# The delta rule's inverse: its transposed form made by TensorE transposes that ScalarE drains, the last level over 64 rows, and the steps of the whole kernel in another order

## The chip, the cores and the metric

One program on one core of a Trainium2 chip. The metric is the device time of one execution in microseconds; a time is the median of several executions. The engines are named TensorE (PE in the profile; its weight loads PEld), VectorE (DVE), ScalarE (ACT), GpSimd (POOL) and SyncE (SP, which issues the DMAs).

## The reference

Two blocks of two layers each, on a sequence of 256 rows of 1024 numbers, float32. A layer of block one has one wide projection, an attention branch with a choice of 64 keys, a gated delta rule branch, a gated sum of both and an output projection. Block two has four small attention branches and a layer norm. The change is in the delta rule. Its core, for each head and each chunk:

```python
kb = k * beta[..., None]
lower = jnp.where(strict, jnp.einsum('bhnid,bhnjd->bhnij', kb, k) * decay, 0.0)
tmat = jnp.eye(CHUNK, dtype=jnp.float32) + lower
u = lax.linalg.triangular_solve(tmat, v * beta[..., None], left_side=True,
                                lower=True, unit_diagonal=True)
w = lax.linalg.triangular_solve(tmat, kb * jnp.exp(gc)[..., None], left_side=True,
                                lower=True, unit_diagonal=True)
...
def step(state, xc):
    qk_c, qd_c, kd_c, u_c, w_c, gt_c = xc
    v_new = u_c - jnp.einsum('bhcd,bhde->bhce', w_c, state)
    o_c = (jnp.einsum('bhcd,bhde->bhce', qd_c, state)
           + jnp.einsum('bhij,bhje->bhie', qk_c, v_new))
    state = state * gt_c[..., None, None] + jnp.einsum('bhcd,bhce->bhde', kd_c, v_new)
    return state, o_c
```

There are 8 heads with keys and values of 128. The kernel takes chunks of 128 rows, so it needs the inverse of a unit lower triangular 128x128 matrix for each head, row block and layer: 8 x 2 x 2 = 32 of them.

## The kernel before, in words

Every engine runs one long list of steps. `lanes` writes a list of steps for each lane: "s" loads and splits weights, "m" is the weight matmuls, "a" the delta rule of block one with its norms (the first lane of attentions in block two), "b" the other attention lane, "c" the convolution, "d" and "v" drains of weight tiles, and so on. `ORDER` is a string with one letter for each step, and says from which lane the next step of `PLAN` comes. Each engine walks through the same `PLAN` and does its part of each step, so `ORDER` sets the order on every engine's queue. Waits are on semaphores that count the steps of one kind on one engine.

**Weights.** The weight matmuls are fp32 values split in two: ScalarE rounds a unit of 128x1024 to fp32r (`w_hi`, the helper `A`, line 1278), GpSimd takes the rest (`w_lo`, line 837), and TensorE adds three fp32r products (lines 888, 893 and 900). Their results go to two tiles `bulk` in PSUM, and ScalarE or VectorE drains them. The splits are queued on ScalarE between its other work.

**The chain.** All other work of TensorE writes to two PSUM tiles `chain0` and `chain1`, in turn in the order of the plan (`two_before`). `take(step)` on TensorE waits until the step two before in this order has been drained by the engine that `DRAINER` names. Products of four heads go through `four` (line 977), transposes through `transposes` (line 921, with the identity as the other operand).

**The inverse.** A group g has 4 heads, r is a block of 128 rows. `lt` holds the lower triangular matrices (transposed), `xt` the inverse so far in transposed form and `xx` in plain form. `sub` inverts the blocks of 8 on VectorE, and step x1 (TensorE's transposes, ScalarE's drain) makes `xx` from `xt`. Then four levels n, which join blocks of 8, 16, 32 and 64 (`LEVELS`). In each level invY makes lt*xx on TensorE, and VectorE masks it into `yy` (line 1920). invZ makes two products for each head: the correction of `xx` in columns 0 to 511 of the PSUM tile, and that of `xt` in columns 512 to 1023; VectorE subtracts the one (line 1927) and then the other (line 1929). In the last level only `xt` is needed. The order within a level is Y of both r, then Z of both r. After the last level u, st, ks and o use `xt`: u is the new values, st the state, ks the state's part for the second chunk, o the output. u, st and x1 are drained by ScalarE.

**Around it.** stat and rn norm the rows of q and k, dec makes the decays, kk the products of keys, rep and sub the small inverses. baT, ba_a to ba_c and gc make beta and the summed decays at a layer's start. onorm, mix_b and mix on VectorE and ScalarE follow the last o and give the mixed rows, mT turns them, and the units "o0" and "o1" are the output projection. memT turns the memory input of block two; its DMA is issued by SyncE after o(1,1) of layer 0 was drained (`load_memory`, line 802). In block two, layer 1, the units of the tile h1 run for each half of the rows in an order of their own (`by_half`, `in_turn`).

Of the kernel before, what the change touches and what calls it, by code (L numbers as in the profile page):

```python
# [24 lines left out]
ALU = mybir.AluOpType  # L25
# [3 lines left out]
P = 128  # L29
S = 256  # L30
R = S // P
# [197 lines left out]
def gdn_chain(g):  # L229
# [3 lines left out]
    for n in range(len(LEVELS)):  # L233
        for r in range(R):
            out.append(("invY", g, r, n))
        if n == len(LEVELS) - 1:
            out.append(("kT", g))
        for r in range(R):
            out.append(("invZ", g, r, n))
        if n == 0:  # L240
            out.append(("vT", g))
# [51 lines left out]
def lanes():  # L293
# [20 lines left out]
    "aaaaasamsvamsaasmmsassaaaaacssaccssmmcammcmmcsmasscmscmacamsmcasmssmaadcaasmaassvmamsssbmmacammsmbas"  # L314
    "madsaadsbaamaasmasaaasmaaaasbmamambabsmbsamadsaacsbcbmmsamsscaabmacacscmmascscmsmascammbscamabamcsac"
    "sasamasmdbbammsbmmaxssbmasmmdsbsamssaxsbaaaasdbbmsbbbswmmmaambaaaadwmsbabassmxaamasbbasmsadssabmmbma"
    "madamsawwamwamxsdsabssxsmadmxwxbxaxsbsmmsxxmxmassmvsssvmmmammassaasamasmsdmmssvasaasaccssmmcssmmcamm"
    "mcsamscmcaamcasacsssmmacasasamcmadaamsmavsmmcsasammbbmaaaabsassaasdmaasbdammsaamaasmbsmbsaamsadbmbma"
    "sssaaammsabsmabaacmasacccsmascccbmbsmsmmbbsmbacbsbmamcsaccssmamadaasmasbbamsasssbdmsammmsmsaammmxsaa"
    "dcsbmasassamaxbmwbmamaasbmaadmabsbwsabsasamadasbsdmbmmaaxaasmsaawmbaswmmswaadmsmadsmxxbassxxwxxsxmbb"  # L320
    "ssmmxxssssmmvmvssmaammammdmaasaaammsssssmasdsssmmmsmmmdamasmmamssassaadsdabmsmmasmbbammbbsabmaassdaa"
    "bssmbbmdbsdbsbmamsbvbmambsbsabbsdmmasmdbmsbdsmsbyamsbmmbsymdbbssdydsaymvbsmyysdmymsvydmssdvvsvssvmmm"
    "dmssyssvsssmmmsmmvmymvmvesmsmeesmmmvmmvssmmaaemmmeeaammmmssmssmmassmdmdmssasmsadammsssabmaaammmssbsm"
    "bsddammsbbmabbsmmbsbbsabdsmdbambmsaabmssabbvsambdmabsmbbsmdsbbmsaambmysdmsbdyysmbamysasyvdbdsyydvmmy"
    "ssmvdssmmdvsvmmsmsmvdvsmysmmsvssssmmysvmmsvmeemmevmvmemememm"
# [3 lines left out]
def plan():  # L329
# [17 lines left out]
    "kk": "vector", "rep": "vector", "x1": "scalar", "kT": "vector", "invY": "vector", "invZ": "vector", "vT": "vector",  # L347
# [105 lines left out]
def build(nc, t, out):  # L453
    ctx = ExitStack()
    with ctx:
# [389 lines left out]
        def _(pe):  # L845
            def handlers(p):
# [160 lines left out]
                def invY(g, r, n):  # L1007
# [5 lines left out]
                    four(c, [(lt[:, r, j, :], xx[:, r, j, :]) for j in range(4)]).then_inc(p.done("invY"), 1)  # L1013

                def invZ(g, r, n):
                    c = take("invZ", g, r, n)
                    pe.wait_ge(*p.after("vector", "invY", g, r, n))
                    if n < len(LEVELS) - 1:
                        four(c[:, 0:512], [(xt[:, r, j, :], yy[:, r, j, :]) for j in range(4)])
                    four(c[:, 512:1024], [(yy[:, r, j, :], xt[:, r, j, :]) for j in range(4)]).then_inc(p.done("invZ"), 1)  # L1020
# [228 lines left out]
                def gT(h):  # L1249
# [7 lines left out]
                            invY=invY, invZ=invZ, kq=kq, u=u_, st=st_, ks=ks, o=o_, iT=iT, raw=raw_, qT=qT, kaT=kaT_,  # L1257
# [6 lines left out]
        def _(act):  # L1264
# [15 lines left out]
            def handlers(p):  # L1280
# [14 lines left out]
                def tile_in(name):  # L1295

                    last = max(u for u, x in enumerate(UNITS[p.sec]) if x[0] == name)
# [152 lines left out]

                def u_(g, r):
# [116 lines left out]
                def ln_s(r):  # L1568
                    if r == 0:
# [6 lines left out]
                            stat=stat, rn=rn, dec_b=dec_b, x1=x1, u=u_, st=st_, onorm_a=onorm_a, onorm=onorm, kinorm=kinorm, iT=iT,  # L1576
# [6 lines left out]
        def _(v):  # L1583
            TT, TS, STT = v.tensor_tensor, v.tensor_scalar, v.scalar_tensor_tensor

            def handlers(p):
# [329 lines left out]
                def invY(g, r, n):  # L1916

                    v.wait_ge(*p.after("tensor", "invY", g, r, n))
                    m = cst[:, K_LEVEL + n * P:K_LEVEL + (n + 1) * P]
                    TT(yy[:, r, :, :], heads(half("invY", g, r, n)[:, 0:512]), over(m, 4), ALU.mult).then_inc(p.done("invY"), 1)  # L1920
# [443 lines left out]
```

## Time and profile before

| | |
|---|---|
| median of 3 runs | 1161.22 us (1160.76 to 1161.28) |
| profiled execution | 1163.95 us, span from first to last instruction 1162.1 us |
| granted TensorE clock, mean over the span | 0.979 |
| TensorE busy | 94%, 6482 passes |
| VectorE / ScalarE / GpSimd busy | 59% / 50% / 58% |
| weight matmuls, lines 888 and 900, share of the chain that ended last | 11% and 43% |
| line 977 (`four`), line 921 (`transposes`), share of that chain | 10% and 4% |

How to read it: busy time is a sum of durations with overlaps counted once. TensorE's passes overlap, so the distance between starts, not the duration of one, tells what a pass costs the queue. What stands behind "idle before" is the time that the engine had nothing to run, and what ended it.

### The profile page before, as it was taken

Reading aid. Unit: us, or ns where it says so; the run is one execution under the profiler, and the core shown is the slowest. Engines: PE = TensorE matmul, PEld = TensorE weight load, DVE = VectorE, ACT = ScalarE, POOL = GpSimd, SP = SyncE. Lnnn points to the kernel's source line nnn. Section 1 sums busy time; section 2 is a strip of 40 time slices with the busy share of each in tenths; the row PEclk is TensorE's granted clock in tenths of the full one; section 3 lists DMA queues with packets and bytes.
Section 4 is the critical chain, followed back from the end, with each engine's and each line's share of the span. In section 5 each row is a group of like instructions: output and inputs, shape, how many; then the busy total and the mean of one; then the engine's idle time right before and its main releaser. Section 6 shows DMA issues by size and latency. Waiting matters only on the chain.

```text
span 1162.1 us, 17023 instructions
## 1 busy us (share of the span) xinstructions
PE 1086.8 (94%) x6482; PEld 948.4 (82%) x6482; DVE 684.2 (59%) x1213; ACT 585.9 (50%) x861; POOL 668.7 (58%) x288
## 2 busy tenths in 40 slices
PE   5989999999989999999999998899999879999986
PEld 4978999888868898889988887787887667897865
DVE  3666655787495547546676477506646652665554
ACT  4535145745553465333656275345566433457651
POOL 3746445564466766444765364687445874744584
PEclk9999999999998999999999999999999988999999
DMA  8634334452415554333454332474433554543351
GB/s 277 180 110 141 94 108 118 118 148 78 120 51 196 163 158 143 111 108 110 131 160 127 82 117 93 145 215 121 125 91 109 181 163 145 139 123 107 93 181 55
DMA packets 84447, 152.07 MB, mean 131 GB/s; under 512 B 10576, under 2 KB 16528, under 8 KB 84368
## 3 DMA queue, kind: packets, MB, share of 16 engines
q1 hardware_dynamic: 84368, 151.00, 43.6%
q8 instruction: 52, 0.85, 0.3%
q14 instruction: 27, 0.22, 0.1%
HBM read 149.93 MB, written 1.05 MB: 130 GB/s over the span
## 4 chain that ended last, share of the span: by engine, by line
PE 79%; DVE 10%; ACT 5%; issue 2%; POOL 2%; DMA 1%; POOLq 0%; DVEq 0%; SPq 0%; ACTq 0%
PE bulk L900 43%; PE bulk L888 11%; PE chain L977 10%; PE chain L921 4%; ACT arena L1278 2%; PE bulk L893 2%; POOL w_lo L837 2%; PE chain L1238 1%; PE chain L959 1%; PE chain L1102 1%; ACT w_hi L1278 1%; ACT L1273 1%; PE chain L1219 1%; DVE arena L1758 1%; DVE arena L1671 1%
## 5 line engine op out<-in xcount | busy, mean ns | idle before, releaser
L837 POOL TENSOR_TENSOR w_lo<-raw,w_hi 128x1024 fp32r<-128x1024 f32 (+4 forms) x279 | 654.4, 2361 | 471.5 <-ACT w_hi L1278 471.0
L1278 ACT ACTIVATE w_hi<-raw 128x1024 fp32r<-128x1024 f32 (+4 forms) x279 | 280.1, 1016 | 250.2 <-PE bulk L900 207.8
L900 PE MATMUL bulk<-w_hi,hT_hi 128*128 128x512 f32 (+1 forms) x756 | 308.9, 409 | 13.2 <-DVE arena L1758 7.9
L900 PE MATMUL bulk<-w_hi,hT_lo 128*128 128x512 f32 (+1 forms) x756 | 296.1, 392 | 0.0
L900 PE MATMUL bulk<-w_lo,hT_hi 128*128 128x512 f32 (+1 forms) x756 | 295.6, 391 | 0.0
L900 PEld LDWEIGHTS bulk<-w_hi,hT_hi 128*128 128x128 f32 x756 | 143.6, 190 | 47.8 <-DVE arena L1758 10.7
L900 PEld LDWEIGHTS bulk<-w_hi,hT_lo 128*128 128x128 f32 x756 | 143.0, 189 | 30.4
L900 PEld LDWEIGHTS bulk<-w_lo,hT_hi 128*128 128x128 f32 x756 | 143.8, 190 | 26.7 <-issue 1.2
L977 PE MATMUL chain<-arena 128*128 128x128 f32 x1056 | 131.3, 277 | 5.6 <-ACT arena L1278 3.6
L977 PEld LDWEIGHTS chain<-arena 128*128 128x128 f32 x1056 | 126.2, 192 | 11.3 <-issue 3.9
L888 PE MATMUL bulk<-hT_hi,w_hi 128*128 128x256 f32 x384 | 112.0, 292 | 0.0
L888 PE MATMUL bulk<-hT_hi,w_lo 128*128 128x256 f32 x384 | 110.0, 287 | 0.0
L888 PE MATMUL bulk<-hT_lo,w_hi 128*128 128x256 f32 x384 | 109.8, 286 | 0.0
L1278 ACT ACTIVATE arena<-chain 128x512 f32<-128x512 f32 (+3 forms) x64 | 46.8, 748 | 100.4 <-PE chain L921 72.7
L1273 ACT ACT_TABLE_LOAD x54 | 69.3, 1283 | 45.6 <-DVE tiny L2099 13.5
L921 PE MATMUL chain<-cst,arena 128*128 128x128 f32 (+2 forms) x512 | 72.7, 282 | 20.3 <-DVE arena L1685 11.5
L921 PEld LDWEIGHTS chain<-cst,arena 128*128 128x128 f32 (+2 forms) x512 | 61.4, 146 | 30.6 <-issue 15.1
L888 PEld LDWEIGHTS bulk<-hT_hi,w_hi 128*128 128x128 f32 x384 | 74.9, 195 | 1.1 <-issue 1.0
L888 PEld LDWEIGHTS bulk<-hT_lo,w_hi 128*128 128x128 f32 x384 | 74.9, 195 | 0.0
L888 PEld LDWEIGHTS bulk<-hT_hi,w_lo 128*128 128x128 f32 x384 | 74.8, 195 | 0.0
L1278 ACT ACTIVATE arena<-bulk 128x1024 f32<-128x1024 f32 (+2 forms) x50 | 50.4, 1007 | 47.3 <-PE bulk L900 47.1
L1776 DVE SCALAR_TENSOR_TENSOR arena<-bulk,par,arena 128x253 f32<-128x253 f32 (+2 forms) x144 | 59.4, 475 | 22.5 <-ACT arena L1278 19.4
(244 smaller groups left out, 1378.4 us busy)
## 6 DMA issues: line engine op xcount, KB each, us to landing
raw<-in_w_in_dram SPq DMA_DIRECT2D x194, 512.0 KB, 3.6
raw<-in_w_out_dram SPq DMA_DIRECT2D x32, 512.0 KB, 4.4
raw<-in_w_branch_dram SPq DMA_DIRECT2D x16, 512.0 KB, 3.8
raw<-in_w_mem_kv_dram SPq DMA_DIRECT2D x8, 512.0 KB, 3.8
raw<-in_w_merge_up_dram SPq DMA_DIRECT2D x16, 256.0 KB, 2.7
raw<-in_w_in_dram SPq DMA_DIRECT2D x8, 420.0 KB, 3.3
gain<-in_ln_rows_dram SPq DMA_DIRECT2D x4, 512.0 KB, 5.2
gain<-in_gains_dram SPq DMA_DIRECT2D x3, 512.0 KB, 6.5
```

The lines of the kernel that those rows point to most:

```text
L837: pool.tensor_tensor(lo_of(p, u)[:, 0:n], raw_of(p, u)[:, 0:n], hi_of(p, u)[:, 0:n].bitcast(F32), ALU.subtract).then_inc(p.done("split"), 1)
L888: m = pe.matmul(dst, a, b[:, kk, :], start=(kk == 0 and i == 0 and j % 2 == 0), stop=(kk == tot - 1 and i == 2 and j % 2 == 1), skip_group ...
L893: m = pe.matmul(pair[0:n, 0:S], a[:, k, :], b[:, kk, :], start=(kk == 0 and i == 0), stop=(kk == tot - 1 and i == 2))
L900: m = pe.matmul(dst, a, b[:, k, :], start=(first and k == 0 and i == 0), stop=(last and k == nk - 1 and i == 2))
L921: m = pe.transpose(c[0:n, i * P:i * P + v.shape[0]], v, ident[0:v.shape[0], 0:v.shape[0]])
L959: m = pe.matmul(c[:, r * 4 + j:r * 4 + j + 1], sq[:, j, r * P:(r + 1) * P], ones[:, 0:1], start=(r == 0 and j == 0), stop=(r == 1 and j == ...
L977: m = pe.matmul(c[:, j * P:(j + 1) * P], a, b, start=(j == 0), stop=(j == 3), skip_group_check=True)
L1102: m = pe.matmul(c[:, j * P:(j + 1) * P], pt[qb][:, i * P:(i + 1) * P], pq[:, k, 1280 + kv * P:1280 + (kv + 1) * P], start=(j == 0 and k == ...
L1219: m = pe.matmul(c[:, q * S:q * S + nk], head_T(n, h, 0, slice(qb * P, (qb + 1) * P)), head_T(n, h, 1, slice(0, nk)), start=(q % 2 == 0), s ...
L1273: act.preload_act_table_set(sets[func])
L1278: return act.activation(dst, src, func, **more)
L1776: ins = STT(cv[:, j, back:S], b[:, j * S:(j + 1) * S - back], par1[:, p.l, c:c + 1], cv[:, j, back:S], ALU.mult, ALU.add)
```

## The change

- invZ makes one product for each head instead of two: only `xx` is corrected (levels 0 to 2), and its PSUM columns 0 to 511 are used alone.
- `xt` of the next level is made from `xx` by a new step invT: four transposes on TensorE, drained by a copy on ScalarE into `xt`. invT of level n-1 stands behind invY of level n in lane "a", for each r, and invZ of a level waits for it. 24 steps are added, 1160 become 1184, and they take their turn at the two PSUM tiles.
- The last level: invY contracts over the first 64 rows and VectorE masks the lower 64 partitions alone; invZ contracts over the upper 64 rows, and VectorE subtracts in the one quarter of `xt` that changes.
- ScalarE's drain of a weight tile waits for the unit that is last in its own order (`in_turn`), which differs for h1 in layer 1 of block two.
- `ORDER` is another string as a whole.

```diff
--- before.py
+++ after.py
@@ -233,6 +233,8 @@
     for n in range(len(LEVELS)):
         for r in range(R):
             out.append(("invY", g, r, n))
+            if n:
+                out.append(("invT", g, r, n - 1))
         if n == len(LEVELS) - 1:
             out.append(("kT", g))
         for r in range(R):
@@ -311,18 +313,18 @@
 
 
 ORDER = (
-    "aaaaasamsvamsaasmmsassaaaaacssaccssmmcammcmmcsmasscmscmacamsmcasmssmaadcaasmaassvmamsssbmmacammsmbas"
...
+    "aaaaaasmvaassasamaaaassmsascmmmcmsscmascacmccsmmascmassmamcsammcsaasmcmdsaassmaaamscsmmvsmdaambssmaa"
...
 )
 
 
@@ -344,7 +346,7 @@
-    "kk": "vector", "rep": "vector", "x1": "scalar", "kT": "vector", "invY": "vector", "invZ": "vector", "vT": "vector",
+    "kk": "vector", "rep": "vector", "x1": "scalar", "kT": "vector", "invY": "vector", "invZ": "vector", "invT": "scalar", "vT": "vector",
@@ -1010,14 +1012,25 @@
                         pe.wait_ge(*p.after("scalar", "x1", g, r))
                     else:
                         pe.wait_ge(*p.after("vector", "invZ", g, r, n - 1))
-                    four(c, [(lt[:, r, j, :], xx[:, r, j, :]) for j in range(4)]).then_inc(p.done("invY"), 1)
+                    if n < len(LEVELS) - 1:
+                        four(c, [(lt[:, r, j, :], xx[:, r, j, :]) for j in range(4)]).then_inc(p.done("invY"), 1)
+                    else:
+                        four(c, [(lt[0:P // 2, r, j, :], xx[0:P // 2, r, j, :]) for j in range(4)]).then_inc(p.done("invY"), 1)
 
                 def invZ(g, r, n):
                     c = take("invZ", g, r, n)
                     pe.wait_ge(*p.after("vector", "invY", g, r, n))
+                    if n:
+                        pe.wait_ge(*p.after("scalar", "invT", g, r, n - 1))
                     if n < len(LEVELS) - 1:
-                        four(c[:, 0:512], [(xt[:, r, j, :], yy[:, r, j, :]) for j in range(4)])
-                    four(c[:, 512:1024], [(yy[:, r, j, :], xt[:, r, j, :]) for j in range(4)]).then_inc(p.done("invZ"), 1)
+                        four(c, [(xt[:, r, j, :], yy[:, r, j, :]) for j in range(4)]).then_inc(p.done("invZ"), 1)
+                    else:
+                        four(c, [(yy[P // 2:P, r, j, :], xt[P // 2:P, r, j, :]) for j in range(4)]).then_inc(p.done("invZ"), 1)
+
+                def invT(g, r, n):
+                    c = take("invT", g, r, n)
+                    pe.wait_ge(*p.after("vector", "invZ", g, r, n))
+                    transposes(c, [xx[:, r, j, :] for j in range(4)]).then_inc(p.done("invT"), 1)
 
                 def kq(g, r):
                     c = take("kq", g, r)
...
@@ -1294,7 +1307,7 @@
 
                 def tile_in(name):
 
-                    last = max(u for u, x in enumerate(UNITS[p.sec]) if x[0] == name)
+                    last = in_turn(p.sec, p.l, name, R - 1)[-1]
                     act.wait_ge(*o.after("tensor", *last_mm(p.sec, p.l, last)))
                     return bulk_of(p, name), dict(TILES[p.sec])[name]
 
@@ -1448,6 +1461,10 @@
                 def half(*key):
                     return chain[half_of[(p.sec, p.l) + key]]
 
+                def invT(g, r, n):
+                    act.wait_ge(*p.after("tensor", "invT", g, r, n))
+                    A(xt[:, r, :, :], heads(half("invT", g, r, n)[:, 0:512]), ACT.Copy).then_inc(p.done("invT"), 1)
+
                 def u_(g, r):
                     act.wait_ge(*p.after("tensor", "u", g, r))
                     A(uu[:, r, :, :], heads(half("u", g, r)[:, 0:512]), ACT.Copy).then_inc(p.done("u"), 1)
...
@@ -1917,6 +1934,12 @@
 
                     v.wait_ge(*p.after("tensor", "invY", g, r, n))
                     m = cst[:, K_LEVEL + n * P:K_LEVEL + (n + 1) * P]
+                    if n == len(LEVELS) - 1:
+                        low = slice(P // 2, P)
+                        TT(yy[low, r, :, :], heads(half("invY", g, r, n)[low, 0:512]), over(m[low, :], 4), ALU.mult).then_inc(
+                            p.done("invY"), 1)
+                        v.wait_ge(*p.here("invY"))
+                        return
                     TT(yy[:, r, :, :], heads(half("invY", g, r, n)[:, 0:512]), over(m, 4), ALU.mult).then_inc(p.done("invY"), 1)
                     v.wait_ge(*p.here("invY"))
 
@@ -1924,9 +1947,10 @@
                     v.wait_ge(*p.after("tensor", "invZ", g, r, n))
                     c = half("invZ", g, r, n)
                     if n < len(LEVELS) - 1:
-                        TT(xx[:, r, :, :], xx[:, r, :, :], heads(c[:, 0:512]), ALU.subtract).then_inc(p.own, 1)
-                        v.wait_ge(*p.last())
-                    TT(xt[:, r, :, :], xt[:, r, :, :], heads(c[:, 512:1024]), ALU.subtract).then_inc(p.done("invZ"), 1)
+                        TT(xx[:, r, :, :], xx[:, r, :, :], heads(c[:, 0:512]), ALU.subtract).then_inc(p.done("invZ"), 1)
+                    else:
+                        up, q = xt[0:P // 2, r, :, P // 2:P], heads(c[0:P // 2, 0:512])[:, :, P // 2:P]
+                        TT(up, up, q, ALU.subtract).then_inc(p.done("invZ"), 1)
                     v.wait_ge(*p.here("invZ"))
 
                 def kq(g, r):
```

## Rows read from the trace of the kernel before

**Rows 1.** The page's first part: busy us (share of the span), instructions

```profile
PE 1086.8 (94%) x6482; PEld 948.4 (82%) x6482; DVE 684.2 (59%) x1213; ACT 585.9 (50%) x861; POOL 668.7 (58%) x288
```

**Rows 2.** The page's fourth part: the chain that ended last, by engine

```profile
PE 79%; DVE 10%; ACT 5%; issue 2%; POOL 2%; DMA 1%; POOLq 0%; DVEq 0%; SPq 0%; ACTq 0%
```

**Rows 3.** Busy time by window, the first and last stretch with inverses (x is instructions)

```profile
core 0: us, PE busy (x) PEld busy (x) DVE busy (x) ACT busy (x) POOL busy (x), PEclk, DMA share, GB/s
107.00:161.00 54.00, 53.32 (x398) 49.73 (x397) 26.60 (x54) 18.08 (x23) 23.67 (x10) 1.00 0.32 93
...
614.00:683.00 69.00, 68.90 (x436) 61.07 (x435) 37.73 (x63) 37.62 (x64) 28.41 (x12) 1.00 0.35 100
```

**Rows 4.** TensorE's timeline: start us, us, instruction, count; layer 0, group 0

```profile
119.13 1.04 PE L921 MATMUL chain<-cst,arena 128*128 128x128 f32 x8
120.00 1.06 PE L977 MATMUL chain<-arena 128*128 128x128 f32 x8
...
123.64 4.63 PE L977 MATMUL chain<-arena 128*128 128x128 f32 x40
...
152.27 1.71 PE L1066 MATMUL chain<-arena 64*128 64x128 f32 x16
153.91 1.16 PE L977 MATMUL chain<-arena 128*128 128x128 f32 x8
```

**Rows 5.** Instructions of lines 977 and 921: durations ns min/median/max, first and last start

```profile
L977 PE MATMUL chain<-arena x1056: 271/275/378, 80.5 to 706.0; 128*128 128x128 f32 x176
...
L921 PE MATMUL chain<-cst,arena x512: 223/273/475, 11.3 to 1135.2; 128*128 128x128 f32 x157, 128*96 128x128 f32 x11, 72*128 72x72 f32 x3
```

**Rows 6.** Groups by shape: busy us, mean ns | idle before us

```profile
L1278 ACT ACTIVATE arena<-chain 128x512 f32<-128x512 f32 x34 | 20.0, 595 | 71.3 <-PE chain L921 43.7 <-PE chain L977 27.6
...
L1927 DVE TENSOR_TENSOR arena<-arena,chain 128x512 f32<-128x512 f32 x24 | 16.5, 687 | 33.1 <-PE chain L977 33.0
```

**Rows 7.** TensorE's timeline at the start of two inverses

```profile
110.81 5.74 PE L977 MATMUL chain<-arena 128*128 128x128 f32 x48
116.31 0.48 PE L900 MATMUL bulk<-w_hi,hT_hi 128*128 128x512 f32 x1
...
471.55 1.03 PE L921 MATMUL chain<-cst,arena 128*128 128x128 f32 x8
...
472.93 5.26 PE L977 MATMUL chain<-arena 128*128 128x128 f32 x43 [0.34 <-ACT arena L1278]
```

**Rows 8.** TensorE's timeline: invY(1,1,3), ks(1), st(0) and ks(0), idle before in brackets

```profile
294.91 1.13 PE L977 MATMUL chain<-arena 128*128 128x128 f32 x8 [1.11 <-DVE arena L1929]
...
324.61 1.13 PE L977 MATMUL chain<-arena 128*128 128x128 f32 x8 [0.78 <-ACT arena L1278]
...
537.51 1.13 PE L977 MATMUL chain<-arena 128*128 128x128 f32 x8 [0.89 <-ACT arena L1278]
...
539.42 1.13 PE L977 MATMUL chain<-arena 128*128 128x128 f32 x8 [0.78 <-ACT arena L1278]
```

**Rows 9.** Timeline at layer 0's start: baT on TensorE, the end of ba_c on VectorE

```profile
22.27 0.32 PE L921 MATMUL chain<-cst,arena 72*128 72x72 f32 x2 [0.60 <-DVE arena L1706]
...
25.09 2.38 DVE L1810 TENSOR_TENSOR tiny<-tiny 128x16 f32<-128x16 f32 x1
```

**Rows 10.** Timeline at layer 0's end: o(1,1), memory DMA's issue, memT(0), mT(1)

```profile
336.52 1.95 PE L977 MATMUL chain<-arena 128*128 128x128 f32 x16
...
344.41 0.37 SPq L802 DMA_DIRECT2D arena<-in_mem_dram  x1
...
349.67 1.97 PE L921 MATMUL chain<-cst,arena 128*128 128x128 f32 x8 [3.49 <-DMA arena<-in_mem_dram]
...
363.12 1.07 PE L921 MATMUL chain<-cst,arena 128*128 128x128 f32 x8
```

**Rows 11.** Windows of TensorE around one fall of the clock: busy (x), clock, DMA

```profile
188.00:191.00 3.00, 2.86 (x25) 1.00 0.11 14
191.00:194.40 3.40, 3.40 (x18) 0.50 0.80 245
```

**Rows 12.** Who waited for whom: us in total, times, longest us

```profile
ACT arena L1278 <- PE chain L921: 72.7, 28, 8.6
...
PE chain L977 <- ACT arena L1278: 3.6, 5, 0.9
```

More of the change, by code:

```diff
@@ L313 @@
 ORDER = (
-    "aaaaasamsvamsaasmmsassaaaaacssaccssmmcammcmmcsmasscmscmacamsmcasmssmaadcaasmaassvmamsssbmmacammsmbas"
[L315 to L323, printed above, removed]
@@ L324 @@
-    "bsddammsbbmabbsmmbsbbsabdsmdbambmsaabmssabbvsambdmabsmbbsmdsbbmsaambmysdmsbdyysmbamysasyvdbdsyydvmmy"
-    "ssmvdssmmdvsvmmsmsmvdvsmysmmsvssssmmysvmmsvmeemmevmvmemememm"
+    "aaaaaasmvaassasamaaaassmsascmmmcmsscmascacmccsmmascmassmamcsammcsaasmcmdsaassmaaamscsmmvsmdaambssmaa"
+    "smasaaaabsmaabmaamaasabmsddasmaasaamasmaaamsaaaacamsacbabsaascmabbsmsmsbcamcssmccsmcmbmsamccamsabbsm"
+    "sccbbadmbmabaaamssxsmbaaassmsmmaabmwdmssdbsmaaambasmbssabmasasbmaamsdmbabamsasabaasamadsbsbbamaawxaa"
@@ new lines @@
+    "mswmxaswamsmdamsadssaamamabswxxaamdmaxassmaxwbxxbsxbxsmmxsmasmmvsmssvamammaassasmsamsmvdmassaamsmasc"
+    "cmsascmsacmscmsmmcacasmcmsamascmassaaamcsamcsaasmdammammssmasaavcsmsaaadsabmbaamasamassamaamasabmaas"
+    "aasamdsaaasamamdamabsamcmsbabasacsmscambcacmsbbmmcassmcsxcsbmaccambbsmcbascamamsaasssasmmbadssbmbass"
+    "mmasbdasmdsmmmbmaaambaawmaasabmsaamabaadssaaasaabbmawsambxaaambssbmabsbmdassbsmwaamxmbasasdmwmambasa"
+    "dmwsambsxxawsmsdbxmxxsmxsmxxxmssvvmsssmmmammmasaasasasmadassmsmmssmmdmbmssmssamdmsssmdmamamsasssbmba"
@@ L326 @@
+    "dmssmmsasbdbabmsbmmmdaaabsdmababsbsambbmsaabsmsbvbabmbysdsmambmbdsaasmbsbmsbamdsmyambdyssmvdsbyymdsb"
+    "ymmyvdyvsvsmdvssmvvsdsmmsmsmmdsmysmssvmmsysmsvvmseesevmsmmmmssmmmmavammmeeeaamsmsmmssdsmssmmsmmmdsms"
+    "dsmbmmsmabambmssadmbmbsmasamsasadambbsbaadmaabbsdbasmbbmamsbavsbmssbabsmsbdmambdmsbdssasmbmbamyabsmy"
+    "ddssmyabbsyysmdvdmybmsmsdyvyssmvmmvmsmsvmvmdssdmvsysmssmsmvyssvveseemmmvmmmvemmmeemm"
 )
@@ L1256, in handlers @@
                             p2T=p2T, pv2=pv2, yT=yT, gT=gT, mm=mm, memT=memT, hT=hT, cwT=cwT, gc=gc_, stat=stat, dec=dec, kk=kk, rep=rep, x1=x1, kT=kT, vT=vT,
-                            invY=invY, invZ=invZ, kq=kq, u=u_, st=st_, ks=ks, o=o_, iT=iT, raw=raw_, qT=qT, kaT=kaT_,
+                            invY=invY, invZ=invZ, invT=invT, kq=kq, u=u_, st=st_, ks=ks, o=o_, iT=iT, raw=raw_, qT=qT, kaT=kaT_,
                             sc=sc, pT=pT, pv=pv, mT=mT)
@@ L1575, in handlers @@
                             split=split, drain_s=drain, tap=conv_tap, conv=conv_silu, norm=norm, ba_b=ba_b, gc_b=gc_b,
-                            stat=stat, rn=rn, dec_b=dec_b, x1=x1, u=u_, st=st_, onorm_a=onorm_a, onorm=onorm, kinorm=kinorm, iT=iT,
+                            stat=stat, rn=rn, dec_b=dec_b, x1=x1, invT=invT, u=u_, st=st_, onorm_a=onorm_a, onorm=onorm, kinorm=kinorm, iT=iT,
                             raw=raw_, qT=qT, kaT=kaT_, sc=sc, pT=pT, tables=tables)
```

## The prediction

> **What bounds the kernel now.** I read the page first. TensorE is busy 94% of the span, VectorE 59%, ScalarE 50%, GpSimd 58% [rows 1], and the chain that ended last is TensorE for 79% [rows 2]. Then the stage table, for the four stretches in which the inverses are made (x1 to u, for two layers and two groups of heads): TensorE is busy in 53.3 of 54 us in the first and 68.9 of 69 in the last, with the full clock granted, VectorE in half of them [rows 3]. So here TensorE's queue sets the time: weight matmuls are laid between the steps of the inverse, what the inverse takes off that queue is time, and VectorE's and ScalarE's work costs only where TensorE has to wait for it.
>
> **What the edit does to TensorE's queue.** Start times, not durations, price a pass, because passes overlap. From 123.64 on, 40 passes of the inverse's matmuls run without a wait and end 4.63 us later; less the last one's own 0.28 that is 4.35/39 = 0.112 us each. Eight transposes start at 119.13 and the next work at 120.00: 0.109 us each [rows 4]. The code makes 528 products through `four` (33 calls of four for each layer and group), and the trace has 1056 passes on its line; it makes 512 transposes out of the arena through `transposes`, and the trace has 512 [rows 5]. So an fp32 product is two passes, 0.223 us, and a transpose one, 0.109 us.
> For each layer, group and row block, 8 in all, the old inverse has 16 products in invY and 8+8+8+4 = 28 in invZ. The new one has 16 in invY, 16 in invZ and 3 x 4 = 12 transposes. Twelve products become twelve transposes: 96 x (0.223 - 0.109) = **10.9 us less** on TensorE. The last level's products contract over 64 rows. The trace has such passes, 16 in the 1.64 us from 152.27 to 153.91, 0.103 each, one change of row half among them [rows 4]; 128 passes by 0.009 would give 1.1 us, none would give 0, I take 0.5.
> **VectorE** loses 24 subtractions of 0.69 us and half of the eight last ones, about 18.5 us; **ScalarE** gets 24 drains of 0.60 us, 14.3 us [rows 6]. Both have room [rows 3], so the first is no gain by itself. It can take away stalls like the 1.1 us before invY(1,1,3), which waited for the second of VectorE's two subtractions [rows 8]: I take 1 us, between 0 and 3.
>
> **What it puts in TensorE's way.** All steps of the chain share two PSUM tiles in turn, and `take` makes each wait until the step two before it is drained; everything behind it on TensorE, weight matmuls too, waits as well. 24 short steps of 0.44 us (four transposes) now stand among steps of 0.90 us (eight passes). The price of a hand-over is in the trace: two x1 steps start at 471.55, eight passes, and the next user of the first tile starts at 472.93 where it could at 472.42, **0.51 us late**, with 0.44 us of work between. With 0.90 us between it is some 0.1 us: the 48 passes from 110.81 to 116.31 hold two such hand-overs and take 5.50 where 48 x 0.112 = 5.37 [rows 7]. So the round trip is about 1.0 us, and TensorE waits for what the work between does not fill.
> I counted both orders by hand, work between a step's end and the step two after it, a stall handed on to the next. In the inverse the old order has one gap of 0.44 and 19 of about 0.9; the new one ten of 0.44 (Y, T, Z or Y, T, Y with no weight unit between, as invY(0,1,2), invT(0,1,1), invZ(0,0,2)) and thirty of 0.9. Over block one it makes 10.5 us against 3.2: **+7.3 us**, between 4 (drains come early) and 10. The count of the new order holds st and ks at 0.5 each; the waits of 0.9, 0.8 and 0.8 us that three of them have now, because they stand right behind what they need [rows 8], are beyond the old count and go: -2.5.
> invZ now also waits for ScalarE's drain of invT of the level before. Between the two the new order has 1.8 to 9 us of TensorE's work, so 0.60 with one weight split (1.06) ahead on ScalarE fits nearly everywhere: 0 to 2 us, I take 0.5. The drain of h1 waits for another unit of the same tile, 1.4 us later, with nobody behind it in need: 0.
>
> **What the new order moves elsewhere.** gc of layer 0 follows baT after 2.9 us of TensorE's work, before after 8.6; its input is there 4.9 us after baT, because an operation on 16 numbers took 2.38 us there [rows 9]: +2 us, or 0 if it is quick. At the end of layer 0, o(1,1) ends on TensorE at 338.5; the DMA of the memory input goes out at 344.41, when VectorE has drained it, TensorE waits for it until 349.67, and mT(1) starts at 363.12 [rows 10], 24.6 us after o, 15.3 of them work. In the new order VectorE has mix(0) behind it, and the DMA goes out 3.4 us after o; then 5.3 until it is there, memT and its drain 3.5, and gmul, pv, onorm, mix_b, pv and mix, which stand behind it, about 11: mT(1) 23.3 us after o, with 12.6 of work. 10.7 us lost, not 9.3: +1.4. Before block two 8.2 us, not 10.9, cover the last norm, and the weight unit comes back between the xT steps: +0.5. sub of layer 0, group 0 has 5.5 us of work beside it, not 8.2: +0.5. Together +4.4, but each hangs on when VectorE is held up; I take **+3**, between -1 and +6. In block two the order near the merges and at the end is nearly the same: 0, 2 either way.
>
> **Sum:** -10.9 - 0.5 - 1 + 7.3 - 2.5 + 0.5 + 3 = **-4.1 us**. The profiled execution took 1163.95 us, its span 1162.1; the median of the runs is 1161.22. The difference is carried over as it is: a span of 1158.0, a median of **1157.1**.
>
> **A rule that speaks against it.** Transposes take 0.109 us here, at a granted clock of 1.00 in stretches that hold many groups of them [rows 3, 4]. The Trainium skill, page "TensorE: Matmul & The Clock Gate", section on PE-mode transpose, gives about 275 ns for one of 128x128 within a kernel, and says that they don't count as activity for the clock. By that price, as an estimate, 96 of them are 26 us against the 21 of the products that go, and the kernel gets slower; the trace disagrees on the price.
>
> **Rivals.**
> (1) *The hand-overs are filled.* VectorE, with 18 us less to do, is early, and the count is half as large: -10.9 - 0.5 - 1 + 3.5 - 2.5 + 0.5 + 0 = -10.9, **1150.3**. For it: TensorE is busy 98% in these stretches. Against it: the 0.51 us came with an idle ScalarE. Chance 0.17.
> (2) *Hand-overs and the order take it all:* 10 and 5 in place of 7.3 and 3, **1161.8**, within 0.2%. For it: the count has 40 short gaps where there were 20. Chance 0.19.
> (3) *Slower: ScalarE's drain is late.* Of the old inverse only x1 waits for ScalarE; 24 steps more do now. With a split (1.06 us) or a table load ahead, the tile comes back that much late. The sum passes +2.3 once the 24 drains are 0.27 us late on average; with a split ahead of half of them it is 24 x 0.53 = 12.7 us, **1165 to 1170**. Against it: ScalarE is the one that waits, 72.7 us before its drains of transposes, and TensorE has waited 3.6 us for ScalarE in `four` [rows 12]. Chance 0.11.
> (4) *Slower: the clock falls.* It fell at 191.0 although TensorE was busy 2.86 of the 3 us before; the 3.4 us at half clock did 18 passes where 3.0 us at full clock had done 25 [rows 11], about 1.5 us lost. Two such falls in each stretch, by half-us waits and transposes, are 8 x 1.5 = 12 us: **1169**. Against it: the stretches hold transposes now and show 1.00 [rows 3]. The page named above has a rule that would do it. Chance 0.04.
> (5) *It doesn't do what it says,* a transpose being two passes: the counts exclude it [rows 5].
>
> **Chances and range.** Forecast 0.49, rivals 0.17, 0.19, 0.11, 0.04. A measurement of this kernel can tell about 0.2%, 2.3 us, from no change. Faster than 1158.9: forecast and (1), 0.66. Same: 0.19. Slower: 0.15. The range leaves out the most of (3) and (4) and little of (1): 1150.5 to 1163.5.
>
> **What would show it.** On `four`'s line 1056 - 192 = 864 passes, 512 + 96 = 608 transposes; 0.112 and 0.109 us unchanged. TensorE's waits in the inverse up by 4 to 10 us, mostly at steps around an invT. A wait before gc near 28 us. VectorE 18 us less busy, ScalarE 14 more. If a pass over 64 rows is much shorter than 0.11, if drains of invT wait behind splits, or if the granted clock falls in these stretches, the sum is wrong there.

## The result and the profile after

The changed kernel took **1167.24 us** (1164.22 to 1168.4) against 1160.99 for the kernel before beside it: ratio 1.0056, 95% interval 1.0041 to 1.0071. The forecast was 1157.1 with a range up to 1163.5. It is 6.3 us slower, where 3.9 us faster was forecast. One of the six runs of the kernel before took 1563.27 us, a slow one, and is not in the ratio.

The page and the shapes of the kernel after; its profiled execution took 1168.40 us, its span 1166.6:

```profile
PE 1087.4 (93%) x6386; PEld 942.2 (81%) x6386; DVE 656.0 (56%) x1189; ACT 588.5 (50%) x878; POOL 664.9 (57%) x288
PE 80%; DVE 11%; ACT 4%; issue 2%; POOL 1%; DMA 1%; POOLq 0%; DVEq 0%; SPq 0%; ACTq 0%
```

Against [rows 1, 2], VectorE is 28 us less busy, and TensorE has 96 passes fewer and is as busy as before: 93% of a longer span. By line and shape (busy us, mean ns, idle before):

```profile
L979 PE MATMUL chain<-arena 128*128 128x128 f32 x736 | 96.9, 280 | 3.5 <-ACT arena L1291 1.5 <-DVE arena L1943 1.2 <-DVE tiny L1886 0.4
L979 PE MATMUL chain<-arena 64*128 64x128 f32 x128 | 18.3, 284 | 0.5 <-DVE arena L1939 0.3 <-ACT arena L1291 0.2
L1291 ACT ACTIVATE arena<-chain 128x512 f32<-128x512 f32 x58 | 33.8, 594 | 106.1 <-PE chain L923 83.4 <-PE chain L979 22.4
L1943 DVE TENSOR_TENSOR arena<-chain,cst 128x512 f32<-128x512 f32 x24 | 16.6, 692 | 39.1 <-PE chain L979 38.9
L1939 DVE TENSOR_TENSOR arena<-chain,cst 64x512 f32<-64x512 f32 x8 | 5.6, 695 | 15.4 <-PE chain L979 15.3
```

Line 979 (977 before) has 736 + 128 = 864 passes, ScalarE 24 drains more (58, where [rows 6] has 34) of the same 0.59 us. The last level's mask over 64 partitions takes as long as one over 128: 695 ns against 692.

The stretches with the first and the last inverse (engines' busy us and instructions, granted clock, DMA), against [rows 3]:

```profile
core 0: us, PE busy (x) PEld busy (x) DVE busy (x) ACT busy (x) POOL busy (x), PEclk, DMA share, GB/s
107.60:160.00 52.40, 51.88 (x377) 47.83 (x376) 20.31 (x52) 19.32 (x27) 23.61 (x10) 1.00 0.36 106
617.80:686.00 68.20, 66.79 (x406) 57.50 (x404) 38.77 (x72) 32.24 (x63) 30.57 (x13) 1.00 0.34 99
```

No loss of six microseconds is to be seen in these two. TensorE's timeline (start, us, idle before in brackets) has larger waits outside the inverse that the kernel before doesn't have: gc of layer 0, then in layer 1 of block one dec, rep, mT(1) and the third matmul step of the memory unit.

```profile
28.49 0.95 PE L949 MATMUL chain<-tiny,cst 128*128 128x8 f32 x4 [2.05 <-DVE tiny L1827]
440.52 0.68 PE L969 MATMUL chain<-cst,tiny 128*128 128x128 f32 x4 [2.46 <-DVE tiny L1855]
463.18 1.10 PE L993 MATMUL chain<-arena,cst 128*128 128x512 f32 x2 [1.62 <-DVE arena L1894]
730.36 0.85 PE L923 MATMUL chain<-cst,arena 128*128 128x128 f32 x6 [2.83 <-DVE arena L2152]
755.55 0.80 PE L902 MATMUL bulk<-w_hi,sT_hi 128*128 128x512 f32 x1 [3.48 <-POOL w_lo L839]
```

A measure for the whole trace: the distance from each pass's start to the next, less the median distance for its line and shape. Summed over all passes this is TensorE's idle and slowed time. The medians alone add up to 1041.7 us before and 1029.9 after, 11.8 less, so the passes saved are there in full. The rest went from 100.3 to 116.7 us: 16.4 more. Below, "idle time" is this sum.

### The profile page after: what moved, and what is told of

The parts are those of the page before. It is cut to its first block, busy times and chain, and to the rows that moved or that the text cites. A ratio compares the mean times of both kernels' runs of the same rounds, so it can differ in the third digit from the quotient of the medians.

```text
span 1166.6 us, 16851 instructions
## 1 busy us (share of the span) xinstructions
PE 1087.4 (93%) x6386; PEld 942.2 (81%) x6386; DVE 656.0 (56%) x1189; ACT 588.5 (50%) x878; POOL 664.9 (57%) x288
## 4 chain that ended last, share of the span: by engine, by line
PE 80%; DVE 11%; ACT 4%; issue 2%; POOL 1%; DMA 1%; POOLq 0%; DVEq 0%; SPq 0%; ACTq 0%
PE bulk L902 45%; PE bulk L890 11%; PE chain L979 8%; PE chain L923 6%; ACT arena L1291 2%; POOL w_lo L839 1%; PE chain L1251 1%; PE chain L961 1%; PE bulk L895 1%; ACT w_hi L1291 1%; PE chain L1115 1%; PE chain L1099 1%; DVE arena L1775 1%; DVE arena L1884 1%; PE chain L1232 1%
## 5 line engine op out<-in xcount | busy, mean ns | idle before, releaser
L1291 ACT ACTIVATE arena<-chain 128x512 f32<-128x512 f32 (+3 forms) x88 | 60.2, 705 | 118.6 <-PE chain L923 95.9
L979 PE MATMUL chain<-arena 128*128 128x128 f32 (+1 forms) x864 | 114.8, 280 | 4.0 <-ACT arena L1291 1.7
L979 PEld LDWEIGHTS chain<-arena 128*128 128x128 f32 (+1 forms) x864 | 106.1, 192 | 14.4 <-ACT arena L1291 3.4
L923 PE MATMUL chain<-cst,arena 128*128 128x128 f32 (+2 forms) x608 | 86.4, 282 | 23.7 <-DVE arena L1702 11.3
L923 PEld LDWEIGHTS chain<-cst,arena 128*128 128x128 f32 (+2 forms) x608 | 72.5, 145 | 34.9 <-issue 18.4
```

Source lines behind the costliest of these rows:

```text
L923: m = pe.transpose(c[0:n, i * P:i * P + v.shape[0]], v, ident[0:v.shape[0], 0:v.shape[0]])
L979: m = pe.matmul(c[:, j * P:(j + 1) * P], a, b, start=(j == 0), stop=(j == 3), skip_group_check=True)
L1291: return act.activation(dst, src, func, **more)
```

## The experiments

The change has three parts: the transposes (invT in place of the second product), the last level over 64 rows, and the order. The first two together are called the form. ScalarE's other wait for h1 comes with the changed form in every run and was not tried alone. An order can be cut at a step: up to it the steps of one order, then all that are left in the other.

**1. Form and order apart.** The old order needs places for invT, and one drain had to move. As steps of the plan (in the kernel they are letters of the string `ORDER`):

```diff
 invY(g, r, n)
+invT(g, r, n-1)        # n = 1, 2, 3: directly behind, no weight unit between
...
-drain_s zb0            # layer 1
 invY(1, 1, 3)
+invT(1, 1, 2)
+drain_s zb0
```

> The whole edit of the inverse (invT steps, last level over 64 rows) in the order of the kernel before; each invT stands directly behind the invY that precedes it, and one drain (zb0 of layer 1) moves back by two steps. Order theory (the form gains what was computed, 11.7 us of TensorE's passes less by the two traces, and the loss of the changed kernel comes from its order): 1148 to 1154 us. Form theory (the hand-overs of the PSUM tiles or ScalarE's drains cost more than the passes save; here 24 gaps of four transposes stand with no weight unit ahead of them): 1163 us or more.

Measured 1165.53 us against 1160.95, ratio 1.0043 (1.0030 to 1.0057). The order theory missed by 11 us: the form alone, in the old order, costs 4.6.

The opposite: the old form, with the new order less its 24 invT steps.

> The inverse as it was before (two products for xx and xt, no invT, whole last level), all steps in the changed kernel's order with the 24 invT steps left out. Order theory: slower than the changed kernel, 1172 to 1179 us, since the order costs some 17 us and the form gives 11 back. Form theory: within 3 us of the kernel before, 1158 to 1164 us.

1170.17, ratio 1.0088 (1.0071 to 1.0106): the order alone costs 9.2 us. Both theories are half right. The two costs don't add up to the 6.3: on the changed form the new order costs only 1.7 us (1167.24 against 1165.53), and TensorE's idle time in the inverse, summed as in the section on the prediction, is 22.2 us in form_old_order and 13.7 in the changed kernel: the new order also fills hand-overs (part 3).

**2. The order by blocks**, with the changed form: old in block one and new in block two, and the mirror.

> The changed form; the order of the kernel before through block one, the changed kernel's order from the first xT of block two on. The two traces have the changed kernel 9.3 us late at the start of block two and 4.5 to 6 us late at the end. If the loss is block one's order, this is the form in the old order and some 3 to 5 us off that: 1145 to 1151 us. If the order of block two costs too, 1152 us or more.

> The mirror of the run before: the changed kernel's order through block one, the old order in block two, with the changed form. Loss in block one's order: 1168 to 1173 us, slower than the changed kernel's 1167.2. Loss in block two's order: 1157 to 1163 us.

1165.62 (1.0039, 1.0023 to 1.0054) and 1172.56 (1.0105, 1.0089 to 1.0120). The first was expected at 1145 to 1151 us if the loss was block one's order; it is as slow as form_old_order. Block two's new order gives 5.3 us behind the new block one and nothing behind the old one. Block one's new order, with the old block two, costs 7.0 (1172.56 against 1165.53), so what the order loses it loses there.

**3. Hand-overs.** The two PSUM tiles hold 1024 columns each, and most steps of the chain write 512 or fewer. Used as four parts, they take away what makes `take` wait:

```diff
...
-            half[step] = len(seen) % 2
-            had[step] = seen[-2] if len(seen) >= 2 else None
-            seen.append(step)
+            sets = [(b,) for b in range(4)] if step[2] in NARROW_STEPS else [(0, 1), (2, 3)]
+            banks = min(sets, key=lambda s: max(last.get(b, (-1, None))[0] for b in s))
+            half[step] = banks
+            had[step] = sorted({last[b] for b in banks if b in last})
...
```

> The changed form in the old order (1165.5 us), and the chain's two PSUM tiles of 1024 columns used as four parts of 512: a step that writes 512 columns or fewer (x1, kk, kT, invY, invZ, invT, kq, u, st, ks, kaT, pv, xT) takes the part that has been free longest, so it waits for the drain of a step about four before it, not two. Hand-over theory (the 0.4 to 0.6 us waits at the step behind each invT, 15.1 us of added idle and 11.7 of saved passes): 1151 to 1156 us. Data theory (the steps wait for their own inputs, drains that are late in any tile): 1162 us or more.

**1152.76** (0.9931, 0.9907 to 0.9954), 12.8 us off form_old_order. The same two steps, invY(0,1,2) and invT(0,1,1) of layer 0, and invZ(0,0,2) behind them, first in form_old_order and then with four parts (TensorE's timeline):

```profile
131.15 1.06 PE L979 MATMUL chain<-arena 128*128 128x128 f32 x8
132.04 0.60 PE L923 MATMUL chain<-cst,arena 128*128 128x128 f32 x4
133.06 1.38 PE L979 MATMUL chain<-arena 128*128 128x128 f32 x10 [0.42 <-DVE arena L1943]
```

```profile
128.20 1.06 PE L987 MATMUL chain<-arena 128*128 128x128 f32 x8
129.09 0.60 PE L931 MATMUL chain<-cst,arena 128*128 128x128 f32 x4
129.53 2.37 PE L987 MATMUL chain<-arena 128*128 128x128 f32 x17
```

From the transposes' start to the next step 1.02 us there and 0.44 here: 0.58 lost to one hand-over, the 0.51 of [rows 7]. This invZ reads the mask of row block 0, long done; what it waited for is the PSUM tile of invY(0,1,2), which VectorE drains on line 1943. Idle time in the four stretches of the inverse, from x1 to u, went from 28.9 to 16.3 us, over the kernel from 115.2 to 100.8.

> The changed kernel (1167.2 us) with the same four parts of PSUM. Its stretches of the inverse hold 3.6 us more idle TensorE than the same order without invT. Hand-over theory: 1161 to 1165 us. If most of the loss is the order elsewhere (waits at dec, rep, mT, the memory unit's split), it stays at 1163 or more. Data theory: 1166 to 1168 us.

1156.68 (0.9975, 0.9953 to 0.9997), 10.5 us off the changed kernel where 2 to 6 were expected. Its idle time falls by 11.9 us, of which 5.2 are in the inverse's stretches. The other 6.7 are spread over steps outside them; which hand-overs those are was not taken apart.

> The kernel before, form and order unchanged, with the four parts of PSUM (its invZ of levels 0 to 2 needs a whole tile). Control: what the parts give without the changed form. Hand-over theory: 1157 to 1161 us (st, ks and the like wait for data, few gaps are short here). If the parts give as much here as in the changed form (10 us), 1151 us, they are a gain of their own and say nothing on invT.

1159.30 (0.9994, 0.9975 to 1.0013). No gain that can be told from none: the parts are worth much where short steps stand behind each other, and little in the old form.

> The changed form in the old order with two PSUM tiles; 31 weight matmul steps inside the inverse's stretches move by a few places, so that a weight unit stands next to most invT. A count of hand-overs at 1.02 us each gives 8.8 us of stalls in the four stretches in place of 15.2 in the old order with each invT directly behind its invY, and 6.7 for the kernel before. Hand-over theory: 1157 to 1161 us. Data theory or late ScalarE drains: 1164 us or more.

**1183.13** (1.0205, 1.0168 to 1.0242), 18 us slower than form_old_order: a plain miss. The count of hand-overs looked at nothing else, and these rows of it did not exist in form_old_order:

```profile
310.76 0.50 PE L902 MATMUL bulk<-w_hi,hT_hi 128*128 128x512 f32 x1 [2.45 <-ACT arena L1291]
348.25 0.66 PE L923 MATMUL chain<-cst,arena 128*128 128x128 f32 x2 [3.72 <-DVE arena L2152]
371.50 0.74 PE L923 MATMUL chain<-cst,arena 128*128 128x128 f32 x5 [2.79 <-DVE arena L2152]
```

A weight unit came in front of the drain of its bulk tile, and mT(0) and mT(1) at layer 0's end wait for mix. It rules out nothing on hand-overs; it shows that moving weight units is no free way to fill them.

**4. Who drains invT.**

```diff
...
-A(xt[:, r, :, :], heads(half("invT", g, r, n)[:, 0:512]), ACT.Copy)...   # ScalarE
+v.tensor_copy(xt[:, r, :, :], heads(half("invT", g, r, n)[:, 0:512]))... # VectorE
...
```

> The changed form in the old order, two PSUM tiles (1165.5 us), with the copies of invT made by VectorE in place of ScalarE. Late ScalarE (splits and table loads ahead of the drain): 1158 to 1162 us. Hand-over theory (the tile comes back a round trip after the four transposes whoever drains it, and the wait is mostly for VectorE's drain of the invY before): 1165 to 1169 us, VectorE having 24 more operations in its way.

1165.63 (1.0042, 1.0026 to 1.0057), the same as with ScalarE in the same old order. It is not the choice of ScalarE that costs there. In the changed kernel itself this was not tried; its trace has TensorE waiting 1.7 us in `four` for ScalarE, less than the 3.6 of [rows 12].

**5. Where the order costs**, with the old form, so that no hand-over of invT is in it.

> The kernel before (old form of the inverse), with the changed kernel's order of steps in layer 0 of block one alone, the old order from the first hT of layer 1 on. The traces of the old form in either order have 0.8 us less idle TensorE at that place in the new order. Order theory (the loss of 9 us sits in layer 1): 1158 to 1162 us. If the order costs evenly over both layers: 1165 us.

> The mirror: the kernel before with the changed kernel's order in layer 1 of block one alone (from its first hT to the first xT of block two). By the traces idle TensorE grows by 12 us there. Order theory: 1168 to 1174 us. If it costs evenly: 1165 us.

1162.85 (1.0013, 1.0003 to 1.0024) and 1176.14 (1.0138, 1.0115 to 1.0162). Layer 0 costs 2 us, layer 1 15. Then layer 1 in parts:

> The kernel before (old form) with the changed kernel's order only in the front of layer 1 of block one, from its first hT to its first x1. With the whole layer 1 in the new order TensorE's idle time grew by 5.9 us there: a wait of 2.62 us at dec for rn, one of 1.78 at rep for VectorE, two clock falls. Waits theory: 1165 to 1169 us. If these waits only stand in place of later ones: 1160 to 1163 us.

1167.77 (1.0070, 1.0049 to 1.0090), 7.2 us. The profiled execution (1165.88) is one of the two fastest of the six, and shows 3.2 of them as idle time in the front; the rest of the 7.2 is in no wait of the front that it shows. The wait at dec is in it, 2.46 us before 438.27. What makes it is on VectorE. These are the last steps of rn, which dec needs, in the kernel before and in the changed one, each with GpSimd's rows of that time:

```profile
438.04 0.17 DVE L1833 TENSOR_SCALAR tiny<-tiny 128x8 f32<-128x8 f32 x1
438.24 0.16 DVE L1836 TENSOR_TENSOR tiny<-tiny 128x4 f32<-128x4 f32 x1
438.44 0.16 DVE L1838 TENSOR_TENSOR tiny<-tiny 128x4 f32<-128x4 f32 x1
...
440.52 8.92 POOL L837 TENSOR_TENSOR w_lo<-raw,w_hi 128x1024 fp32r<-128x1024 f32 x4 [6.37 <-ACT w_hi L1278]
```

```profile
435.53 2.39 DVE L1850 TENSOR_SCALAR tiny<-tiny 128x8 f32<-128x8 f32 x1
437.95 0.16 DVE L1853 TENSOR_TENSOR tiny<-tiny 128x4 f32<-128x4 f32 x1
438.14 2.23 DVE L1855 TENSOR_TENSOR tiny<-tiny 128x4 f32<-128x4 f32 x1
...
435.48 7.18 POOL L839 TENSOR_TENSOR w_lo<-raw,w_hi 128x1024 fp32r<-128x1024 f32 x3 [4.19 <-ACT w_hi L1291]
```

An operation on eight numbers for each partition takes 0.17 us while GpSimd rests, and 2.39 us, the length of one split (7.18 / 3), when it starts as GpSimd's splits run. rn as a whole takes 1.6 us before and 5.9 after. The same slow operation is in the trace of new_front1_old_form:

```profile
433.28 2.39 DVE L1833 TENSOR_SCALAR tiny<-tiny 128x8 f32<-128x8 f32 x1
435.70 0.16 DVE L1836 TENSOR_TENSOR tiny<-tiny 128x4 f32<-128x4 f32 x1
435.90 2.23 DVE L1838 TENSOR_TENSOR tiny<-tiny 128x4 f32<-128x4 f32 x1
```

The Trainium skill, page "GPSIMD Engine Reference", section "Key points", says that GpSimd shares its SBUF interfaces with VectorE, and that VectorE's instructions in a 2-port mode or with two SBUF inputs contend. The 2.23 us of the TENSOR_TENSOR agree; which of the two cases the TENSOR_SCALAR is, with one tensor as input, the rows don't show.

The new order has no more such collisions than the old one: 62 VectorE operations took over 0.8 us more than the shortest of their line and shape, where there were 65, and every one of them, in both traces, ran beside an instruction of GpSimd. It has them at another place. The kernel before has the same collision at dec of layer 0, where the changed kernel has none (TensorE first, then the end of rn):

```profile
71.53 1.83 PE L967 MATMUL chain<-cst,tiny 128*128 128x128 f32 x7 [3.76 <-DVE tiny L1838]
...
65.36 2.38 DVE L1833 TENSOR_SCALAR tiny<-tiny 128x8 f32<-128x8 f32 x1
67.77 2.26 DVE L1836 TENSOR_TENSOR tiny<-tiny 128x4 f32<-128x4 f32 x1
70.06 1.32 DVE L1838 TENSOR_TENSOR tiny<-tiny 128x4 f32<-128x4 f32 x1
```

That wait changes from execution to execution (3.76 us here and in form_old_order, 1.10 in new_layer1_old_form, all with the same order up to there), while the one at layer 1's dec is 2.46 us in the changed kernel and in the three old-form traces with the new front. That nothing but GpSimd makes these operations slow was not tried alone.

> The kernel before (old form) with the changed kernel's order only from u of row block 1, group 1, layer 1, to the first xT of block two. In the whole new layer 1 idle TensorE grew by 8.8 us between these: mT(1) waits 4.74 us for mix, the memory unit's second matmul 3.64 us for GpSimd's split. Waits theory: 1168 to 1172 us. If the waits come from what the order does further ahead in the layer (splits and loads late at entry to the tail): 1160 to 1164 us.

1168.08 (1.0064, 1.0051 to 1.0077), 7.5 us; about 8 by the idle time in the trace. The waits of the changed kernel are there, with the old form and an old front:

```profile
723.20 1.06 PE L921 MATMUL chain<-cst,arena 128*128 128x128 f32 x8 [2.87 <-DVE arena L2128]
748.45 0.79 PE L900 MATMUL bulk<-w_hi,sT_hi 128*128 128x512 f32 x1 [3.48 <-POOL w_lo L837]
```

Front and tail, 7.2 + 7.5 us, are the 15.2 of the layer within the noise. The tail's two waits are for VectorE's mix and for a split of GpSimd; what makes those late was not taken apart. And in the changed kernel:

> The changed kernel, two PSUM tiles, with the old order (each invT directly behind its invY) in layer 1 of block one alone. If layer 1's order is the loss, its 15 us go, but the hand-overs that this order has with invT (9.6 us over its two stretches by the idle time in form_old_order) come: 1161 to 1165 us. If the loss of the changed kernel is spread: 1166 us or more.

1162.08 (1.0015, 1.0004 to 1.0027): 5.2 us come back when layer 1 alone has its old order, although the dense hand-overs come with it.

**6. The 64 rows.** In the fastest version so far (four parts, old block one, new block two) this was to size a term of half a microsecond:

> Candidate: the changed form, four parts of PSUM, the old order through block one and the changed kernel's order in block two. Form in the old order with four parts is 1152.8. The order of block two took 5.4 us off behind the new block one and nothing off behind the old one. If what it saves (the wait for the last norm before xT of layer 1, 7.0 against 3.0 us) is real: 1148 to 1151 us. If it is given back: 1152 to 1154 us.

1151.27 (0.9917, 0.9904 to 0.9930). With the whole last level again, on TensorE as shown and in VectorE's mask and subtraction too:

```diff
...
-four(c, [(lt[0:P // 2, r, j, :], xx[0:P // 2, r, j, :]) for j in range(4)])
+four(c, [(lt[:, r, j, :], xx[:, r, j, :]) for j in range(4)])
...
-four(c, [(yy[P // 2:P, r, j, :], xt[P // 2:P, r, j, :]) for j in range(4)])
+four(c, [(yy[:, r, j, :], xt[:, r, j, :]) for j in range(4)])
...
```

> The fastest version so far (four parts of PSUM, old order in block one, new in block two, 1151.3 us) with the last level over all 128 rows as before: 128 passes over 64 rows more become passes over 128, VectorE's last mask and subtraction are whole. If passes over 64 rows are 0.009 us shorter, and VectorE's halves hide: 1151.5 to 1153.5 us. If the 64 rows give more (a shorter VectorE drain ahead of a waiting step): 1154 us or more.

**1148.08** (0.9897, 0.9880 to 0.9913), the fastest kernel of all: both theories had it slower, and it is 3.2 us faster (2.3 by the two ratios). In the changed kernel and in the one before:

> The changed kernel (1167.2 us), its last level over all 128 rows again, on TensorE and VectorE. In the fastest version this change gave 3.2 us: by its two traces a first pass behind a change between 64 and 128 rows starts 0.202 us after the one before, in place of 0.112, and 0.202 in place of 0.030 ahead of a weight pass, while passes over 64 rows take the same 0.112. Theory of the change of rows (32 such changes at 0.09 to 0.17 us, and the hand-overs behind them): 1162 to 1165 us. If the gain in the fastest version was another thing (its clock falls, its hand-overs with four parts): 1166 us or more.

> The kernel before with the last level of its inverse over 64 rows as in the changed kernel, and nothing else. Theory of the change of rows: 1163 to 1166 us against 1160.6 to 1161. By the prediction's term (passes over 64 rows 0.009 us shorter, VectorE's half operations): 1159.5 to 1161 us.

1161.13 (1.0009, 0.9991 to 1.0026), 6.1 us off the changed kernel, more than expected, with runs from 1157.98 to 1166.05; and 1163.73 (1.0024, 1.0009 to 1.0039) for the 64 rows alone, 3.5 us above the 1160.23 beside it. So the 64 rows cost in all three pairs, between 2 and 6 us. TensorE's timeline around invY(0,0,3) and invY(0,1,3) of layer 0, changed kernel first, then with the whole level:

```profile
142.61 0.28 PE L890 MATMUL bulk<-hT_hi,w_lo 128*128 128x256 f32 x1
142.82 1.16 PE L979 MATMUL chain<-arena 64*128 64x128 f32 x8
143.90 0.39 PE L890 MATMUL bulk<-hT_hi,w_hi 128*128 128x256 f32 x1
...
146.88 0.60 PE L923 MATMUL chain<-cst,arena 128*128 128x128 f32 x4
147.41 1.16 PE L979 MATMUL chain<-arena 64*128 64x128 f32 x8
148.50 0.65 PE L923 MATMUL chain<-cst,arena 128*128 128x128 f32 x4
148.91 0.36 PE L890 MATMUL bulk<-hT_hi,w_hi 128*128 128x256 f32 x1
```

```profile
142.69 0.28 PE L890 MATMUL bulk<-hT_hi,w_lo 128*128 128x256 f32 x1
142.81 1.05 PE L979 MATMUL chain<-arena 128*128 128x128 f32 x8
143.62 0.36 PE L890 MATMUL bulk<-hT_hi,w_hi 128*128 128x256 f32 x1
...
146.58 0.60 PE L923 MATMUL chain<-cst,arena 128*128 128x128 f32 x4
147.01 1.06 PE L979 MATMUL chain<-arena 128*128 128x128 f32 x8
147.91 0.61 PE L923 MATMUL chain<-cst,arena 128*128 128x128 f32 x4
148.28 0.36 PE L890 MATMUL bulk<-hT_hi,w_hi 128*128 128x256 f32 x1
```

A change between passes over 128 rows and over 64 costs time on both sides of the step: 0.21 in place of 0.12 us into the first one, 1.08 in place of 0.81 for the eight passes and the way out, 0.53 and 1.09 in place of 0.43 and 0.90 at the second. From the last weight pass to 148.91 it is 6.30 us, to 148.28 5.59: 0.71 for two steps, 0.36 each. Not every step costs that much: the same distances, into the group and from it to the next pass, taken over all 16 steps of the two traces, are 3.9 us longer with 64 rows, 0.24 a step. In the version with four parts it is 2.9 us, in the old form 1.8. The 3.9 is what the trace shows of the 6.1; where the rest comes from stays open. The passes over 64 rows themselves start 0.112 us apart (median), like those over 128. The Trainium skill, page "TensorEngine Tiling (Array Packing)", section "Key Properties", says that changing the tiling mode drains TensorE. The rows agree in that each change between 64 and 128 rows costs; that it is a drain they don't show.

## Why the prediction was wrong

Two terms of the sum failed. The order outside the hand-overs was put at +0.5 and cost 9.2 us, because layer 1's start and end were left out, and the 64 rows were put at -0.5 and cost 2 to 6 us, because the change between 64 and 128 rows was given no price.

Undone in turn, the parts account for the 6.3 us: the order +9.2 (old_form_new_order over before), the transposes -9.0 (after_full_last_level over that), the 64 rows +6.1 (the changed kernel over that). The medians come from three sets of runs with before at 1160.2 to 1161.0, so each is good to about 1.5 us. Another way round gives other shares: 64 rows +3.5, then transposes +1.8 (form_old_order over before_64_rows), then the order +1.7. The first way is compared with the prediction here, because its order term is measured without invT, as the prediction's was.

- **Transposes in place of products, -10.9:** right. 864 and 608 passes, 0.112 and 0.109 us apart; the medians' sum fell by 11.8.
- **Hand-overs, +7.3 between 4 and 10:** the price was right (0.58 measured, 0.51 taken), the count too high for the new order. With VectorE's relief (-1) and the wait for invT (+0.5) the step "transposes" was put at -4.1 and is -9.0, so that by subtraction hand-overs come to some 2 us. The traces say the same of the inverse: from 2.5 us before the first mask of a group to 8 us behind its last, all four groups, TensorE's idle time is 7.4 us before, 11.5 with the new order, 10.9 with the transposes too and 13.7 with the 64 rows. It went up by the 4 to 10 us that the prediction gave as a sign, but not by the transposes. This is what rival (1) said; its total, 1150.3, was off all the same. Where nothing fills the hand-overs they are as bad as feared: the same sum is 9.3 us for before_64_rows and 22.2 for form_old_order, and four parts of PSUM give back 12.8.
- **64 rows, -0.5:** failed, with the sign wrong: +6.1 in the changed kernel, some 3 in the two other pairs. The 0.103 us for a pass was a misread mean. In the trace of the kernel before, the 16 passes from 152.27 to 153.91 start 0.112 us apart where the row half stays, and three of them start under 0.01 us behind a pass on the other half; those pull the mean down, and the inverse's passes have no such neighbour. The cost of the change was in the same passes: the first starts 0.21 us after the weight pass before it and the second 0.21 after that, and behind them the first pass over 128 rows starts 0.20 after the last and the next 0.22 after it. Bounded by "none would give 0", the term left out this loss without a reason.
- **Order elsewhere, +3 between -1 and +6, and the old waits at st, ks and invY, -2.5:** together +0.5, measured +9.2. The wait at gc is there as said (2.05 us at 28.49), and the old waits are gone: none before `four` is over 0.4 us. But the prediction went through the order at layer 0's start and end, and of layer 1 only through its last norm (+0.5). Layer 0 costs 2 us, near the forecast, in part by luck: 3.76 us of wait at its dec, which the prediction didn't have, went away. Layer 1 costs 15, half in its front and half in its tail. In the front the trace shows 2.46 us at dec, from VectorE's small operations under GpSimd's splits. [rows 9] had shown one of those, taken there as a number without a cause. Block two's order gives 5 back behind it. These sizes (2, 15, -5) add up to 12 and not 9.2; they come from different pairs.
- **ScalarE's drain late, rival (3):** excluded by invT_by_vector for the old order, and not seen in the changed kernel's trace. The 1165 to 1170 us it gave hold the result, for another reason: that agreement is luck.
- **Clock, rival (4):** not in the stretches of the inverse, where 1.00 is granted and none of the falls lies. Over the span it is 0.976 against 0.979: eight falls to 0.50 before, eleven after, and in layer 1 three begin right behind the waits shown (441.6, 731.7, 755.6), so that these waits cost more than their own length. By [rows 11] a fall of 3.4 us costs 1.2 us (3.4 less 18 passes of 0.12), not the 1.5 of the prediction.
- **VectorE 18 us less busy, ScalarE 14 more:** 28 less and 3 more. ScalarE's drains are there (24 x 0.59), but the new order has 47 table loads of 1.28 us (line 1286) where the old one has 54 (1273); in form_old_order, with 54, ScalarE is busy 599.4 us, 13.5 more than in [rows 1].

## What to carry to other kernels

Undo a change part by part before believing its story, and from both ends: here the order that looked harmless took 9 us and the 64 rows 2 to 6, and the transposes gave 9 us in the new order and nothing in the old one. Where short steps share buffers in turn, cut the buffers to what a step writes before moving work about to fill the gaps: it gave 12.8 us where moving work lost 18. Don't shrink a few matmuls to half of the rows among full ones (it lost in all three pairs here), and place the small VectorE operations that TensorE waits for where GpSimd rests.

## What was not expected of the hardware

- Half the rows save TensorE nothing (0.112 us between starts either way), and a step of eight such passes among full ones costs more: 0.24 us in the mean of 16 steps, 0.36 in the two shown.
- Passes on different row halves start under 0.01 us behind each other (three of the 16 from 152.27 on, in the kernel before).
- Half the partitions save VectorE nothing: 695 ns for 64x512 against 692 for 128x512.
- A VectorE operation of 0.17 us took 2.39 us beside a GpSimd split of 2.39 us.
